# Writing the residual of an encoder layer to the output early, and adding the final feed-forward result to it by an accumulating DMA

## The chip, the cores and the metric

The kernel runs on the 8 cores of one Trainium2 chip, each core on its own part of the tokens with no exchange between them. The metric is the device time in microseconds of the slowest core. The profile is of one execution, taken on the slowest core of that execution (core 3).

## The reference

```
for l in range(2):                       # DEPTH
  h = rmsnorm(x, g_pre_mix);  u = h @ w_in[l]         # 1024 -> 6144
  y_a = pooled means of four windows, projected, scaled
  y_b = b_gate * dwconv3(c_gate * v)
  m = sigmoid(ga) * y_a + sigmoid(gb) * y_b
  x = x + rmsnorm(m @ w_out[l], g_post_mix)
  f = rmsnorm(x, g_pre_ffn)
  x = x + rmsnorm((silu(f @ w_ffn_gate) * (f @ w_ffn_up)) @ w_ffn_down, g_post_ffn)
```

This is applied to 2 sequences of 8192 tokens and 16 sequences of 2048 tokens, in fp32, with width 1024 and a hidden width of 2816. The rows that matter here are the last two: the residual x after the mixing half is used once to make f and once more at the very end, in the sum.

## The kernel before

Each core takes 6 tiles (the loop over t) of 1024 tokens, with a halo of 16 on either side: 1056 columns, held with the features on the 128 partitions in 8 chunks (k). For each tile both layers (l) are run in full on the chip. The columns are cut into three sub-tiles s of 352. x_t (fp32) holds the residual, h_t (bf16) the normalised input of the matmuls, o_t (fp32) the result of an output projection before its normalisation, m_t (bf16) the mixed values, and R the intermediate values. h_t and m_t are also used as scratch for the squares from which the norms are made.

One layer is: the projections of four groups g (for g = 0 four weight blocks are kept and s is the outer loop, lines 457 to 463), the output projection (lines 524 to 530, s outer), gate and up of the feed-forward (line 534 on; for its first three pairs of weight blocks s is the outer loop, lines 549 to 552, 12 groups of 8 matmuls for each s), and down. The last four column blocks of down (the "tail", lines 585 to 588) have s as the outer loop: 4 groups of 22 matmuls for each s.

Between two halves of a layer stand two chains for each s. chain_A (line 311) closes a half: 8 matmuls with a matrix of ones sum the squares in h_t (rstd_for), ScalarE makes the reciprocal root by Ln and Exp, VectorE multiplies the 8 chunks of o_t by it (mult_r), and VectorE and GpSimd add them to x_t (add_x). Then pre_sq writes the squares of x_t to m_t on ScalarE. chain_B (line 305) opens the next half: 8 matmuls with ones over m_t, Ln and Exp, and 8 scalar_tensor_tensor on VectorE that write h_t.

In the last layer of a tile (final) chain_A adds into o_t instead of x_t, and then, in this order: load_x issues the load of the next tile's x into the same columns of x_t (SP's queue), store_y issues the store of o_t to yout (SP's queue), halo_mask clears halo columns on VectorE (s = 0 and s = 2 only), pre_sq squares the new x, and chain_B is put off. So in the code before, the new x can be loaded only when the old residual has been added.

The chains are woven between the groups of matmuls by a list, pend. defer appends an entry with a number of matmuls to wait for; each main group calls run_pending, which looks at the first entry alone (line 212), runs it when its number has fallen to 0, and lowers the number of all entries by the size of the group. ensure_h(s) (line 206) is called ahead of each group that reads h_t: as long as any entry carries the tag s, it runs entries from the front of the list, whatever their numbers are. Each engine runs its instructions strictly in the order in which they were emitted; waits are semaphores that Sched works out from reads and writes.

The weights are fetched as fp32 and cast to bf16 by DMAs issued from GpSimd's queue into 11 slots; a load is emitted when the unit 11 places earlier is released (release, issue_upto). The tail of down holds 8 slots until rel_tail runs, 40 matmuls after it was deferred. Of the four blocks with which the next tile starts (pool, ga, v, gb), the first three are loaded ahead, and the fourth, gb, is emitted behind chain_A of s = 1.

Of the kernel before, what the change touches and what calls it, by code (L numbers as in the profile page):

```python
# [9 lines left out]
ALU = mybir.AluOpType  # L10
# [3 lines left out]
KC = 8  # L14
FF = 2816
JC = 22
DEPTH = 2
NT = 6
TV = 1024
HALO = 16  # L20
W = TV + 2 * HALO
NSUB = 3
SW = W // NSUB
# [78 lines left out]
def build_nc():  # L102
# [8 lines left out]
    yout = nc.dram_tensor("yout", [NT, 128, KC, TV], F32, kind="ExternalOutput").ap()  # L111

    with contextlib.ExitStack() as es:
# [3 lines left out]
        x_t = sb("x_t", [128, KC, W], F32)  # L117
        h_t = sb("h_t", [128, KC, W], BF16)
        o_t = sb("o_t", [128, KC, W], F32)
# [32 lines left out]
        def emit_all(S, plan, rec):  # L152
            X = [[Buf() for _ in range(NSUB)] for _ in range(KC)]
# [9 lines left out]
            SGB = [Buf() for _ in range(NSG)]  # L163
            CSB = Buf()
            MISC = Buf()

            state = {"bank": 0, "unit": 0, "ln": 0, "sg": 0, "issued": 0, "released": 0}
            pend = []
# [34 lines left out]
            def defer(nmm, fn, tag=None):  # L203
                pend.append([nmm, fn, tag])
# [82 lines left out]
            def load_x(t, s):  # L287
                S.dma("sp", (lambda q, t=t, s=s: q.dma_start(out=x_t[:, :, col(s)],
                                                             in_=xin[t, :, :, s * SW:(s + 1) * SW])),
                      ("xl", s), writes=[X[k][s] for k in range(KC)])  # L290

            def halo_mask(t, s):
                if s == 0:
                    bl = [X[k][0] for k in range(KC)]
                    tsmul(x_t[:, :, 0:HALO], x_t[:, :, 0:HALO], cc(128 + 2 * t), reads=bl + [CSB], writes=bl)
                if s == NSUB - 1:
                    bl = [X[k][NSUB - 1] for k in range(KC)]
                    tsmul(x_t[:, :, W - HALO:W], x_t[:, :, W - HALO:W], cc(128 + 2 * t + 1),
                          reads=bl + [CSB], writes=bl)

            def pre_sq(s):
                for k in list(range(KC // 2, KC)) + list(range(KC // 2)):
                    act(m_t[:, k, col(s)], x_t[:, k, col(s)], AF.Square, reads=(X[k][s],), writes=(M[k][s],))

            def chain_B(s, gbase):
                bi = rstd_for(s, lambda k, s_: m_t[:, k, col(s_)], M)
                for k in range(KC):
                    stt(h_t[:, k, col(s)], x_t[:, k, col(s)], cc(gbase + k), banks[bi][:, 0:SW], ALU.mult, ALU.mult,
                        reads=(X[k][s], BANKB[bi], CSB), writes=(H[k][s],))

            def chain_A(s, t, l, which):
                cb = l * 64
                bi = rstd_for(s, lambda k, s_: h_t[:, k, col(s_)], H)
                final = which == "ffn" and l == DEPTH - 1
                lo = max(s * SW, HALO)
                hi = min((s + 1) * SW, W - HALO)
                def mult_r(k):
                    tt(o_t[:, k, col(s)], o_t[:, k, col(s)], banks[bi][:, 0:SW], ALU.mult,
                       reads=(O[k][s], BANKB[bi]), writes=(O[k][s],))

                def add_x(k, eng):
                    if not final:
                        tt(x_t[:, k, col(s)], x_t[:, k, col(s)], o_t[:, k, col(s)], ALU.add,
                           reads=(X[k][s], O[k][s]), writes=(X[k][s],), eng=eng)
                    else:
                        tt(o_t[:, k, col(s)], x_t[:, k, col(s)], o_t[:, k, col(s)], ALU.add,
                           reads=(X[k][s], O[k][s]), writes=(O[k][s],), eng=eng)

                def store_y():
                    S.dma("sp", (lambda q, t=t, lo=lo, hi=hi: q.dma_start(  # L330
                        out=yout[t, :, :, lo - HALO:hi - HALO], in_=o_t[:, :, lo:hi])),
                          ("st", s), reads=[O[k][s] for k in range(KC)])

                for k in range(KC // 2, KC):
                    mult_r(k)
                    add_x(k, "pool")
                for k in range(KC // 2):
                    mult_r(k)
                    add_x(k, "dve")
                if which == "mix":  # L340
                    gnext = cb + 16
                    nt_ = t
                elif not final:
                    gnext = (l + 1) * 64
                    nt_ = t
                else:
                    if t + 1 >= NT:
                        store_y()
                        return
                    gnext = 0  # L350
                    nt_ = t + 1
                    load_x(nt_, s)
                    store_y()
                if which == "ffn":
                    halo_mask(nt_, s)
                pre_sq(s)
                defer(120 if final else 72, lambda: chain_B(s, gnext), tag=s)

            def out_proj_evac(bi, c, s, gbase):
                act(o_t[:, c, col(s)], banks[bi][:, 0:SW], AF.Copy, reads=(BANKB[bi], CSB), writes=(O[c][s],),  # L360
# [235 lines left out]
            while pend:  # L596
                it = pend.pop(0)
                it[1]()
            S.final_wait("sp", [("st", i) for i in range(NSUB)])

        rec = []
        emit_all(Sched(), None, rec)
# [145 lines left out]
```

How the kernel before makes its waits and increments, by code:

```python
        def run_stream(engine, name):  # L612
            for waits, fn, ikey, iamt in S.streams[name]:
                for key, val in waits:
                    engine.wait_ge(sems[key], val)
                if fn is not None:
                    ins = fn(engine)
                    ins.then_inc(sems[ikey], iamt)
```

## Time and profile before

| | |
|---|---|
| time, median of 2 runs | 6384.32 us (6290.19 and 6478.44) |
| time of the profiled execution | 6289.86 us |
| its span on core 3 | 6288.1 us (cores: 6258.3 to 6288.1) |
| TensorE busy | 5662.1 us, 90% |
| ScalarE / VectorE / GpSimd busy | 3278.4 / 2917.8 / 743.3 us |
| granted TensorE clock, mean | 0.953 |

Busy time is the time in which an engine had an instruction under way. A matmul at the full clock and one at half the clock both count as busy, so a stretch with a low granted clock looks busier than the work in it.

### The profile page before, as it was taken

The numbers are of one execution on the slowest core, as the hardware profiler recorded it, in microseconds if no ns is written. First come the engines' busy times: TensorE is split into PE (matmuls) and PEld (weight loads), VectorE is DVE, ScalarE is ACT, GpSimd is POOL, SyncE is SP. The second block draws the span as 40 slices with busy tenths as digits, with TensorE's granted clock in tenths as the row PEclk, the third lists the DMA queues.
The fourth block names the chain that finished last, engine by engine and source line by source line (L and its number), as shares of the span: only waits on it lengthen the run. The fifth ranks groups of instructions, "written<-read, shape, count | busy, mean of one in ns | idle before, by whom it ended". The sixth has DMA issues, their size and how long they took to land.

```text
span 6288.1 us, 107415 instructions; the slowest of 8 cores (6258.3 to 6288.1 us)
## 1 busy us (share of the span) xinstructions
PE 5662.1 (90%) x36864; PEld 3644.5 (58%) x36864; DVE 2917.8 (46%) x4934; ACT 3278.4 (52%) x6793; POOL 743.3 (12%) x1132
## 2 busy tenths in 40 slices
PE   6999998889989699998968999978899896999999
PEld 3566655556656365665645665645566563656655
DVE  5643542552553264265246436425525633643642
ACT  4564563465555356456435645635655553564564
POOL 0101011010110101101111011010101101011011
PEclk9999999899999899999989999989999997999999
DMA  5334343533434443343353343444334344433532
GB/s 102 63 63 72 62 67 82 92 59 64 74 52 75 100 76 58 58 84 61 65 101 60 63 73 62 68 91 84 61 58 79 60 70 99 68 63 61 84 57 62
DMA packets 159073, 448.39 MB, mean 71 GB/s; under 512 B 14032, under 2 KB 57040, under 8 KB 158544
## 3 DMA queue, kind: packets, MB, share of 16 engines
q0 software_dynamic: 120960, 390.12, 37.7%
q1 hardware_dynamic: 37584, 51.39, 2.5%
q8 instruction: 310, 5.08, 0.3%
q14 instruction: 219, 1.79, 0.1%
HBM read 806.36 MB, written 25.17 MB: 132 GB/s over the span
## 4 chain that ended last, share of the span: by engine, by line
PE 77%; DVE 9%; ACT 7%; DMA 4%; issue 3%; DVEq 0%; ACTq 0%; POOL 0%; SPq 0%; POOLq 0%
PE bank L227 77%; DMA x_t<-xin 4%; DVE o_t L242 4%; DVE h_t L246 3%; ACT m_t L238 2%; DVE x_t L242 2%; ACT sg L238 1%; ACT h_t L238 1%; ACT o_t L238 1%; ACT lnv L238 1%; ACT bank L238 1%; ACT R L238 0%; DVE R L242 0%; DVE m_t L242 0%; DVEq L615 0%
## 5 line engine op out<-in xcount | busy, mean ns | idle before, releaser
L227 PE MATMUL bank<-h_t,slot 128*128 128x352 bf16 x26496 | 4090.7, 318 | 484.9 <-ACT h_t L238 138.4
L227 PEld LDWEIGHTS bank<-h_t,slot 128*128 128x128 bf16 x26496 | 2623.1, 99 | 1935.3 <-issue 517.0
L227 PE MATMUL bank<-R,slot 128*128 128x352 bf16 x6912 | 1045.0, 313 | 0.0
L238 ACT ACTIVATE sg<-bank 128x352 f32<-128x352 f32 x1368 | 627.0, 458 | 529.1 <-DVE sg L242 428.0
L227 PEld LDWEIGHTS bank<-R,slot 128*128 128x128 bf16 x6912 | 676.5, 98 | 355.1
L238 ACT ACTIVATE sg<-sg,onef 128x352 f32<-128x352 f32 x1368 | 804.0, 588 | 128.5 <-ACT sg L238 2.6
L242 DVE TENSOR_TENSOR sg<-bank,sg 128x352 f32<-128x352 f32 x792 | 415.1, 524 | 966.6 <-ACT sg L238 960.2
L238 ACT ACTIVATE o_t<-bank,cs 128x352 f32<-128x352 f32 x576 | 326.2, 566 | 693.7 <-PE bank L227 693.7
L242 DVE TENSOR_TENSOR o_t<-o_t,bank 128x352 f32<-128x352 f32 x576 | 270.8, 511 | 815.6 <-ACT bank L238 815.6
L238 ACT ACTIVATE m_t<-x_t 128x352 bf16<-128x352 f32 x576 | 244.5, 486 | 709.2 <-DVE x_t L251 368.1
L242 DVE TENSOR_TENSOR R<-bank,R 128x352 f32<-128x352 f32 x576 | 281.4, 519 | 606.7 <-PE bank L227 573.9
L246 DVE SCALAR_TENSOR_TENSOR h_t<-x_t,cs,bank 128x352 bf16<-128x352 f32 x576 | 289.6, 575 | 550.4 <-ACT bank L238 522.4
L238 ACT ACTIVATE R<-bank 128x352 f32<-128x352 f32 x576 | 236.1, 461 | 549.6 <-DVE R L242 439.2
L242 DVE TENSOR_TENSOR R<-R 128x1055 f32<-128x1055 f32 (+5 forms) x384 | 428.0, 1115 | 69.3 <-ACT R L238 51.8
L242 DVE TENSOR_TENSOR R<-bank,sg 128x352 bf16<-128x352 f32 x792 | 415.7, 525 | 86.4 <-DVE sg L242 5.1
L238 ACT ACTIVATE sg<-sg 128x352 f32<-128x352 f32 x792 | 393.2, 496 | 74.5 <-ACT sg L238 2.2
L227 PE MATMUL bank<-m_t,slot 128*128 128x352 bf16 x2304 | 371.2, 324 | 50.5 <-DVE m_t L242 37.7
L227 PEld LDWEIGHTS bank<-m_t,slot 128*128 128x128 bf16 x2304 | 230.7, 101 | 187.1 <-issue 58.5
L242 POOL TENSOR_TENSOR x_t<-x_t,o_t 128x352 f32<-128x352 f32 x216 | 224.3, 1065 | 836.8 <-DVE o_t L242 836.8
L238 ACT ACTIVATE R<-sg 128x352 f32<-128x352 f32 x576 | 286.1, 497 | 56.9 <-ACT sg L238 2.2
L181 POOL DMA_DIRECT2D slot<-win x288 | 153.5, 540 | 1336.1 <-PE bank L227 1332.3
L181 POOL DMA_DIRECT2D slot<-wgu x264 | 140.4, 534 | 1397.1 <-PE bank L227 1396.9
(32 smaller groups left out, 1961.0 us busy)
## 6 DMA issues: line engine op xcount, KB each, us to landing
slot<-win POOLq DMA_DIRECT2D x288, 512.0 KB, 6.5
slot<-wgu POOLq DMA_DIRECT2D x264, 512.0 KB, 7.2
slot<-wdd POOLq DMA_DIRECT2D x192, 352.0 KB, 5.6
x_t<-xin SPq DMA_DIRECT2D x18, 1408.0 KB, 10.1
slot<-wod POOLq DMA_DIRECT2D x48, 512.0 KB, 5.6
yout<-o_t SPq DMA_DIRECT2D x12, 1344.0 KB, 13.3
yout<-o_t SPq DMA_DIRECT2D x6, 1408.0 KB, 12.4
slot<-pwd POOLq DMA_DIRECT2D x48, 128.0 KB, 4.0
```

The source lines that it names most:

```text
L181: g.dma_start(out=slots[si][:, 0:nel], in_=src_ap)),
L227: ins = pe.matmul(out_ap, lhsT=l_, rhs=r_, start=(i == 0), stop=(i == n - 1))
L238: a.activation(out=out, in_=in_, func=func, **kw)), reads=reads, writes=writes)
L242: v.tensor_tensor(out=out, in0=in0, in1=in1, op=op)), reads=reads, writes=writes)
L246: v.scalar_tensor_tensor(out=out, in0=in0, scalar=scalar, in1=in1, op0=op0, op1=op1)),
```

## The change

Once chain_B of s has made h_t for the feed-forward of the last layer, a new function after_mid stores x_t of that s to yout, loads the next tile's x into the same columns, and defers (by 220 matmuls, with no tag) the halo mask and the squares of the new x. chain_A of the last layer no longer adds x: it multiplies o_t and then issues, from GpSimd's queue, for each chunk k a DMA that adds o_t to yout in memory. chain_B of the next tile is deferred by 24 matmuls instead of 120. The other places are as before.

```diff
-            def chain_B(s, gbase):
+            def chain_B(s, gbase, after=None):
...
+                if after is not None:
+                    after()
+
+            def after_mid(s, t):
+                lo = max(s * SW, HALO)
+                hi = min((s + 1) * SW, W - HALO)
+                S.dma("sp", (lambda q, t=t, lo=lo, hi=hi: q.dma_start(
+                    out=yout[t, :, :, lo - HALO:hi - HALO], in_=x_t[:, :, lo:hi])),
+                      ("st", s), reads=[X[k][s] for k in range(KC)], writes=(YB[s],))
+                if t + 1 < NT:
+                    load_x(t + 1, s)
+
+                    def nxt(s=s, t=t):
+                        halo_mask(t + 1, s)
+                        pre_sq(s)
+                    defer(220, nxt)
...
+                if final:
+                    for k in range(KC):
+                        mult_r(k)
+                        S.dma("pool", (lambda g_, t=t, k=k, lo=lo, hi=hi: g_.dma_start(
+                            out=yout[t, :, k, lo - HALO:hi - HALO], in_=o_t[:, k, lo:hi], accum_op=ALU.add)),
+                              ("acc", k * NSUB + s), reads=[O[k][s], YB[s]], writes=())
+                    if t + 1 < NT:
+                        defer(24, lambda: chain_B(s, 0), tag=s)
+                    return
...
                 if which == "mix":
                     gnext = cb + 16
-                    nt_ = t
-                elif not final:
+                    aft = (lambda: after_mid(s, t)) if l == DEPTH - 1 else None
+                else:
                     gnext = (l + 1) * 64
-                    nt_ = t
-                else:
-                    if t + 1 >= NT:
-                        store_y()
-                        return
-                    gnext = 0
-                    nt_ = t + 1
-                    load_x(nt_, s)
-                    store_y()
-                if which == "ffn":
-                    halo_mask(nt_, s)
+                    aft = None
+                    halo_mask(t, s)
                 pre_sq(s)
-                defer(120 if final else 72, lambda: chain_B(s, gnext), tag=s)
+                defer(72, lambda: chain_B(s, gnext, aft), tag=s)
...
-            S.final_wait("sp", [("st", i) for i in range(NSUB)])
+            S.final_wait("sp", [("st", i) for i in range(NSUB)] + [("acc", i) for i in range(KC * NSUB)])
```

## Rows read from the trace of the kernel before

**Rows 1.** The page: busy time by engine, and the chain that ended last, by line.
```profile
PE 5662.1 (90%) x36864; PEld 3644.5 (58%) x36864; DVE 2917.8 (46%) x4934; ACT 3278.4 (52%) x6793; POOL 743.3 (12%) x1132
PE bank L227 77%; DMA x_t<-xin 4%; DVE o_t L242 4%; DVE h_t L246 3%; ACT m_t L238 2%; DVE x_t L242 2%; ACT sg L238 1%; ACT h_t L238 1%; ACT o_t L238 1%; ACT lnv L238 1%; ACT bank L238 1%; ACT R L238 0%; DVE R L242 0%; DVE m_t L242 0%; DVEq L615 0%
```

**Rows 2.** Windows, PE: start:end, us, busy (matmuls), clock, DMA share, GB/s.
```profile
1014.20:1150.20 136.00, 78.04 (x456) 0.77 0.44 102
...
5200.00:5330.00 130.00, 72.95 (x399) 0.75 0.46 105
```

**Rows 3.** Timeline, first tile boundary: start, us, engine, what, [idle before <-releaser].
```profile
1018.81 19.85 PE L227 MATMUL bank<-R,slot 128*128 128x352 bf16 x132
...
1069.21 5.37 PE L227 MATMUL bank<-h_t,slot 128*128 128x352 bf16 x24 [13.20 <-ACT h_t L238]
...
1088.53 0.54 SPq L288 DMA_DIRECT2D x_t<-xin  x1
...
1116.23 3.20 ACT L238 ACTIVATE m_t<-x_t 128x352 bf16<-128x352 f32 x8 [37.23 <-DVE x_t L251]
...
1119.92 2.51 PE L227 MATMUL bank<-h_t,slot 128*128 128x352 bf16 x8 [27.20 <-ACT R L238]
```

**Rows 4.** Timeline, layer 0 to layer 1 in the first tile, PE.
```profile
568.90 4.85 PE L227 MATMUL bank<-h_t,slot 128*128 128x352 bf16 x16 [6.19 <-ACT sg L238]
```

**Rows 5.** Timeline, start of the last layer's gate and up, first tile.
```profile
791.88 5.79 PE L227 MATMUL bank<-h_t,slot 128*128 128x352 bf16 x24 [6.26 <-ACT h_t L238]
...
797.50 1.36 PE L227 MATMUL bank<-m_t,ones 128*128 128x352 bf16 x8
...
800.17 4.02 DVE L246 SCALAR_TENSOR_TENSOR h_t<-x_t,cs,bank 128x352 bf16<-128x352 f32 x8 [0.62 <-ACT bank L238]
...
804.11 2.23 DVE L242 TENSOR_TENSOR o_t<-o_t,bank 128x352 f32<-128x352 f32 x5
...
813.62 5.16 PE L227 MATMUL bank<-h_t,slot 128*128 128x352 bf16 x24 [6.41 <-DVE sg L242]
```

**Rows 6.** Timeline, the same stretch: where the chains of s = 0 stand.
```profile
770.36 0.53 DVE L242 TENSOR_TENSOR x_t<-x_t,o_t 128x352 f32<-128x352 f32 x1
...
779.99 4.02 DVE L246 SCALAR_TENSOR_TENSOR h_t<-x_t,cs,bank 128x352 bf16<-128x352 f32 x8 [9.11 <-ACT bank L238]
```

**Rows 7.** The page: DMA queues (packets, MB, share) and issues (KB each, us to landing).
```profile
q0 software_dynamic: 120960, 390.12, 37.7%
q1 hardware_dynamic: 37584, 51.39, 2.5%
...
slot<-win POOLq DMA_DIRECT2D x288, 512.0 KB, 6.5
...
x_t<-xin SPq DMA_DIRECT2D x18, 1408.0 KB, 10.1
yout<-o_t SPq DMA_DIRECT2D x12, 1344.0 KB, 13.3
...
slot<-pwd POOLq DMA_DIRECT2D x48, 128.0 KB, 4.0
```

**Rows 8.** Timeline, end of the last tile, where no x is loaded.
```profile
6246.51 1.36 PE L227 MATMUL bank<-h_t,ones 128*128 128x352 bf16 x8
...
6249.18 2.25 DVE L242 TENSOR_TENSOR o_t<-o_t,bank 128x352 f32<-128x352 f32 x5 [56.35 <-ACT bank L238]
...
6262.03 10.01 PE L227 MATMUL bank<-R,slot 128*128 128x352 bf16 x66
...
6263.50 2.24 DVE L242 TENSOR_TENSOR o_t<-o_t,bank 128x352 f32<-128x352 f32 x5 [8.03 <-ACT bank L238]
...
6275.96 2.24 DVE L242 TENSOR_TENSOR o_t<-o_t,bank 128x352 f32<-128x352 f32 x5 [6.18 <-ACT bank L238]
```

**Rows 9.** Timeline, GpSimd's weight loads at the first tile boundary.
```profile
1054.43 0.57 POOL L181 DMA_DIRECT2D slot<-win  x1
...
1087.93 2.66 POOL L181 DMA_DIRECT2D slot<-win  x5
```

More of the change, by code:

```diff
@@ L165, in emit_all @@
             MISC = Buf()
+            YB = [Buf() for _ in range(NSUB)]
             state = {"bank": 0, "unit": 0, "ln": 0, "sg": 0, "issued": 0, "released": 0}
```

## The prediction

> **What bounds the kernel now.** I read the busy shares first: TensorE 90% busy, no other engine over 52% [rows 1]. So only idle TensorE time, and time at its lower clock, can be won. The chain of waits says where some of it is: 77% TensorE, and 4% the DMA that loads x [rows 1], some 250 us. Then I looked for TensorE's idle times in the timeline. They cluster where one tile ends and the next begins, five times in a run. The first boundary shows the pattern [rows 3]: x is loaded when the old residual has been added (for the third sub-tile its load is issued at 1088.5); ScalarE, which runs in order, stands in front of the squares of the new x while finished banks wait behind them, so TensorE stands for 13.2 us, and for 27.2 us at the third load, whose squares start 27.7 us after its issue. Restarted matmuls are slow: 8 in 2.51 us (0.31 us each), where 132 in a row take 19.85 us, thus (19.85 - 0.31)/131 = 0.149 us each [rows 3]. 352 columns in 0.149 us is the 2.4 GHz level and 0.31 is the 1.2 GHz one.
>
> The whole price of a boundary, idle time and slow clock together, is the length of a window around it less its matmuls at 0.149 us [rows 2]: 136 - 456 x 0.1492 = 68.0 for the first, 130 - 399 x 0.1492 = 70.5 for the fifth, and 67.7, 67.2 and 65.2 for the three between, which look the same. Sum **338.6 us**, 5.4% of the run.
>
> **Part 1: the boundary, -338.6 us.** In the changed kernel the squares of the new x are in m_t before the tail of down. The final chain_A is ones, Ln, Exp, 8 multiplications; it has no add, no squares and no DMA on which ScalarE or VectorE waits. For the timing I use the last tile, which ran without loads [rows 8]. Count from chain_A of s = 0 (ones at 6246.5, called 0): multiplications from +2.7 on; chain_A of s = 1 multiplies from +17.0; the last tail matmul ends at 6272.0, +25.5. The change puts two more ones groups of 1.36 us in here (chain_B of s = 0 and 1, each 2 groups of 22 behind its chain_A), so the next tile's matmuls start at +28.2. h_t of s = 0 must be ready then: its ones start at about +9.3, and from ones to the end of the 8 VectorE instructions is 800.17 + 4.02 - 797.50 = 6.7 us [rows 5], so +16. h_t of s = 1 is ready near +34, needed 8 groups (9.5 us) behind +28.2. For s = 2 chain_A comes after two groups and chain_B at the sixth; h_t is ready near +42, needed at +28.2 + 19.1 + 2.7 = +50. None is late. I take the whole 338.6 as gone and look for what is late next.
>
> **Part 2: GpSimd's queue.** 144 accumulating DMAs are added (8 for each s, 24 a tile), in the place of 72 adds on GpSimd and 72 on VectorE, which were beside TensorE's work. Each waits for its multiplication; five of these take 2.25 us [rows 8], eight 3.7, and the GpSimd adds in the same place waited for the same instructions, so the issue itself costs nothing. What matters is their time in the DMA queue, since the load of block gb is emitted right behind the eight of s = 1 (before, at 1054.4, behind the adds [rows 9]), and seven more loads behind the eight of s = 2. No row shows an accumulating DMA. Let T be the time of the eight (1.4 MB). Lower bound: plain copies, 51.39 MB in 2.5% of 6288 us over 36 DMAs [rows 7], **4.4 us**. Upper bound, if each trip ends before the next starts: 8 x 4.0 us, from the smallest load, pwd [rows 7], 32 us, or 64 us if the read of the destination and the write are a trip each. Deadlines: gb is needed 6 groups into the tile, +28.2 + 7.2 = +35.4, and with a landing time of 6.5 us [rows 7] it comes at +19.1 + T + 6.5; so it is in time up to **T = 9.8**. Above 15.6 the groups queue on each other: gb comes at 9.5 + 2T, late by 2T - 25.9; the block behind it (due at +28.2 + 28.6 + 2.7 = +59.5) adds T - 20.9. Together 3T - 46.8 a boundary. I take T = 8.8, twice the copy, as an accumulation reads two operands and writes one; that it is nearer the copy than the trips is because loads do overlap: five are issued in 2.66 us [rows 9], and 390.12 MB in 37.7% of the span is 3.2 us for the 0.52 MB of a win load, which takes 6.5 us to land [rows 7]. At T = 8.8 gb has 1.0 us to spare. Landing times scatter, so I allow 2.5 us a boundary: **+12.5 us**.
>
> The Trainium skill has a rule against many small DMAs ("DMA: Bandwidth & Descriptors", section on the anatomy of one DMA): about 2.0 us fixed plus bytes/436e3 us. Eight of 176 KB in series would be 19 us, late by 12 us a boundary, 60 us in all; the rows of overlapping loads speak against the series. The skill's "Collectives: The Full Stack" (Part 3, on the bandwidth ceiling) holds that a reduction costs two source reads on one ring and thus halves the rate, not that the add itself is slow, which would be T = 8.8; no row here shows it.
>
> **Part 3: the start of the last layer's gate and up, five tiles.** Here the list works against the change. When chain_B of s = 0 runs, after_mid appends an entry of 220 at the place ahead of chain_B of s = 1, and only the first entry is looked at. So chain_B of s = 1 does not run after 72 matmuls but when ensure_h(1) forces it, at the first group that needs it; ahead of it comes the deferred mask and squares. The same for s = 2. Before, chain_B had its slack (ones at 797.5, eight groups before s = 1) [rows 5]. Now: s = 0 restarts at 791.9 and has 88 matmuls left, 13.1 us plus 2.2 for the slow start (24 in 5.79 us), so it ends at 807.2. ScalarE finishes the last step's three activations (1.6), squares the new x (3.2 [rows 3]), makes the root (1.2), VectorE writes h_t (4.2 with its latency): 10.2 us, of which the two ones groups cover 2.6. **Stall 7.6.** Then chain_A of s = 2 comes right behind and blocks ScalarE's evacuations: in the rows TensorE is released 9.5 us after VectorE starts that chain (804.1 to 813.6) and has 7.2 us of free banks: **2.2**. At s = 2 again 10.2 less one ones group: **8.8**. Sum 18.6; the old stall of 6.41 goes [rows 5]. Net 12.2, and 1.9 for one more slow restart: **14.1 a tile, +70 us in five**. In the sixth tile nothing is deferred by 220 and nothing is lost.
>
> For the loads: the store of s = 0 can go out at 770.9, when the last add is done, and the load at 784, when chain_B has read x [rows 6] and the store (13.3 us [rows 7]) has landed; 10.1 us later it is there, 794, before 807. The load of s = 1 goes out near 817 and is there at 827, needed at 835. The third has 33 us. So SP's queue delays no one; 18 stores moved here and 25 MB of additional traffic find idle DMA engines, and the weight loads are issued from another queue. The other halo_mask and 72-matmul places stay. Two squares groups of 3.2 us move out of the boundary; that of s = 2 lies in steady gate-up work and costs nothing while ScalarE has spare time (1.6 us of activations for 2.4 us of matmuls).
>
> **Part 4: the end.** Before, the span ends 12.1 us behind the first of the last multiplications, at 6276.0 [rows 8], with the adds and one store between. Now the first accumulate goes 0.6 us behind it and the eighth lands some T + 4.0 us later (4.0 the landing of the smallest load [rows 7]): 13.4 for T = 8.8. I count 0 for it; T = 32 makes it +24, T = 64 +56.
>
> **Sum.** 6289.9 - 338.6 + 12.5 + 70 = 6034, **6035 us**, 4.1% under the profiled execution; that execution is the lower of the two runs, 1.5% under their median.
>
> **Rivals.**
> (a) The loads of x land late. If they take the 27 us of the third load in rows 3, the squares forced by ensure_h wait for 784 + 27 = 811, not 807, and for 844, not 835: some 4 + 9 us a tile beyond the sum, 65 us: **6100**. For it: gate-up weight loads are issued about then. Against: in the rows the long landing came with seven weight loads just issued.
> (b) The accumulates are slower than two copies, T = 19: 2 x 19 - 25.9 = 12 a boundary, **6085**. For it: rows of 1.4 KB, read and written. Against: the overlap above.
> (c) A chain remains at the boundary as between layers 0 and 1, where there is no load and TensorE still stands 6.2 us [rows 4] and restarts slowly: some 10 us five times, **6085**. Against: that stall is ScalarE waiting on adds for squares, which this boundary no longer has.
> (d) Each DMA of the eight waits for the one before, T = 32: 49 us a boundary eat the gain of 338.6/5 - 14.1 = 53.6: 6290 - 268.6 + 246 + 24, **6290**, no change.
> (e) On the other side: the read of yout and the write back are each a trip, T = 64, at the same place, GpSimd's DMA queue ahead of gb. 3 x 64 - 46.8 = 145 a boundary against 53.6: 6290 - 268.6 + 727 + 56, **6805**. It turns slower than before at T = 33, and slower by 2% at about T = 42.
>
> **Chances.** Forecast 0.56; (a) 0.13; (b) 0.12; (c) 0.05; (d) 0.07; (e) 0.07. Faster by over 2% (about what a measurement of this kernel can tell from no change): 0.86; within 2%: 0.07; slower: 0.07. The range goes from 5965, where the forced chains of part 3 cost almost nothing (the floor is 6290 - 339 = 5951), to 6200, which takes in (a), (b) and (c) together.
>
> **What would show it.** In the changed kernel's boundary windows the matmuls should fill the time at clock 1.00, with no wait for x_t. At the start of the last layer's gate and up TensorE should show two idle times of 7 to 9 us per tile, released by VectorE's h_t, with 8 squares of m_t just before Ln. The landing time of the accumulates gives T directly; if TensorE waits for a slot or a DMA 6 groups into a tile, (b), (d) or (e) is at work. If ScalarE's m_t waits for the load of x, it is (a). Wrong would be the reading that the load is what costs the 68 us, if the boundary stays above 15 us with neither of these.

## The result

The changed kernel's median is 6199.06 us of 11 runs (6012.7 to 6771.96), that of the kernel before, in the runs taken with it, 6617.88 us of 10 (6287.2 to 7198.04). The ratio of the two is 0.954, 95% interval 0.950 to 0.959. It is taken from runs in which the granted clock of TensorE was about the same on both dies; in the others it was lower on one die or both, whatever the kernel. The profiled execution took 6012.4 us, 277.5 less than that of before (6289.9). The sum of the prediction was 6034. As ratios of the profiled executions: 0.956 measured, 0.959 forecast.

Below, spans and windows are compared on cores whose clock was not lowered, and mostly by one stage: from the start of the output projection of layer 1 to that of layer 0 in the next tile. It holds both places that the change touches. In the changed kernel it begins and ends with the first and the last of these rows of the timeline; the middle one is the first matmul of down (start, us, engine, what, idle before):

```profile
747.45 2.80 PE L228 MATMUL bank<-m_t,slot 128*128 128x352 bf16 x9 [3.14 <-DVE m_t L243]
...
973.73 6.58 PE L228 MATMUL bank<-R,slot 128*128 128x352 bf16 x43
...
1241.96 8.25 PE L228 MATMUL bank<-m_t,slot 128*128 128x352 bf16 x43 [3.15 <-DVE m_t L243]
```

The difference is 494.5 us; the five stages of this profile take 494.1 to 494.5. In the kernel before they took 547.1 to 552.3, mean 549.6. So 55.3 us went from each of five stages, 276 us in all: the whole of what the spans differ by. The other stage, from layer 0 to layer 1, took about 496 us in both.

The first matmul of down parts the two places that the change touches. In the kernel before, the same two rows of the first of the five tiles read

```profile
748.27 11.98 PE L227 MATMUL bank<-m_t,slot 128*128 128x352 bf16 x68 [3.14 <-DVE m_t L242]
...
961.83 13.44 PE L227 MATMUL bank<-R,slot 128*128 128x352 bf16 x89
```

Output projection, gate and up took 213.0 to 213.7 us before and 225.9 to 226.3 after: 12.7 more a tile. Down and the boundary took 333.7 to 339.0 before, mean 336.2, and 268.2 or 268.3 after: 68.0 less.

### The profile page after: what moved, and what is told of

Its sections match the earlier page's. It is cut to its first block, busy times and chain, and to the rows that moved or that the text cites. A ratio compares the mean times of both kernels' runs of the same rounds, so it can differ in the third digit from the quotient of the medians.

```text
span 6010.9 us, 107550 instructions; the slowest of 8 cores (6009.1 to 6010.9 us)
## 1 busy us (share of the span) xinstructions
PE 5621.3 (94%) x36864; PEld 3633.8 (60%) x36864; DVE 2876.1 (48%) x4862; ACT 3281.8 (55%) x6793; POOL 795.5 (13%) x1204
## 3 DMA queue, kind: packets, MB, share of 16 engines
q0 software_dynamic: 141696, 415.30, 43.4%
## 4 chain that ended last, share of the span: by engine, by line
PE 83%; DVE 7%; ACT 6%; issue 2%; DMA 1%; ACTq 0%; DVEq 0%; POOL 0%; SPq 0%; POOLq 0%
PE bank L228 83%; DVE o_t L243 3%; DVE h_t L247 2%; ACT m_t L239 2%; DVE x_t L243 2%; ACT sg L239 1%; ACT h_t L239 1%; DMA x_t<-xin 1%; ACT o_t L239 1%; ACT lnv L239 1%; ACT bank L239 0%; DVE R L243 0%; ACT R L239 0%; DVE sg L243 0%; DVE m_t L243 0%
## 5 line engine op out<-in xcount | busy, mean ns | idle before, releaser
L228 PE MATMUL bank<-m_t,slot 128*128 128x352 bf16 x2304 | 372.0, 324 | 49.9 <-DVE m_t L243 37.7
L182 POOL DMA_DIRECT2D slot<-win x288 | 182.6, 860 | 1137.1 <-PE bank L228 1136.0
```

The lines of the kernel that those rows point to most:

```text
L182: g.dma_start(out=slots[si][:, 0:nel], in_=src_ap)),
L228: ins = pe.matmul(out_ap, lhsT=l_, rhs=r_, start=(i == 0), stop=(i == n - 1))
```

## The profile after

Busy shares, and the chain of work that ended last, by line. Against [rows 1] the load of x has fallen from 4% of the chain to 1%, and TensorE is busy 94% of the time.

```profile
PE 5621.3 (94%) x36864; PEld 3633.8 (60%) x36864; DVE 2876.1 (48%) x4862; ACT 3281.8 (55%) x6793; POOL 795.5 (13%) x1204
PE bank L228 83%; DVE o_t L243 3%; DVE h_t L247 2%; ACT m_t L239 2%; DVE x_t L243 2%; ACT sg L239 1%; ACT h_t L239 1%; DMA x_t<-xin 1%; ACT o_t L239 1%; ACT lnv L239 1%; ACT bank L239 0%; DVE R L243 0%; ACT R L239 0%; DVE sg L243 0%; DVE m_t L243 0%
```

Windows around the first and the last of the five tile boundaries (start:end, us, TensorE busy and matmuls, clock, DMA share, GB/s), to be held against [rows 2]:

```profile
1013.50:1149.50 136.00, 136.00 (x914) 1.00 0.76 112
...
4973.00:5109.00 136.00, 136.00 (x914) 1.00 0.75 112
```

136 us hold 914 matmuls at clock 1.00 where they held 456 at 0.77. 914 x 0.149 = 136: nothing of the 68 us is left, and the three boundaries between read the same (913 or 914 matmuls, clock 1.00). The price is seen in the timeline at the start of the last layer's gate and up:

```profile
791.08 15.33 PE L228 MATMUL bank<-h_t,slot 128*128 128x352 bf16 x88 [6.26 <-ACT h_t L239]
...
806.25 1.36 PE L228 MATMUL bank<-m_t,ones 128*128 128x352 bf16 x8
...
808.64 3.20 ACT L239 ACTIVATE m_t<-x_t 128x352 bf16<-128x352 f32 x8 [1.54 <-DVE x_t L252]
...
812.94 4.02 DVE L247 SCALAR_TENSOR_TENSOR h_t<-x_t,cs,bank 128x352 bf16<-128x352 f32 x8 [4.39 <-ACT bank L239]
...
817.11 17.15 PE L228 MATMUL bank<-h_t,slot 128*128 128x352 bf16 x96 [8.31 <-DVE h_t L247]
...
843.32 6.92 PE L228 MATMUL bank<-h_t,slot 128*128 128x352 bf16 x35 [7.86 <-DVE h_t L247]
```

s = 0 now runs through in 88 matmuls, then come the squares of the next tile's x (808.6), then the VectorE instructions of chain_B, then TensorE's first matmul of s = 1, 8.31 us late; at s = 2 it is 7.86. The old wait of 6.41 [rows 5] is gone. The window 780 to 880 holds 473 matmuls where that of before held 559.

GpSimd's queue at the first boundary: the eight accumulates of s = 1, the load of gb behind them, and the answer for this one load (min/median/max to landing):

```profile
1048.83 7.00 POOL L354 DMA_DIRECT2D yout<-o_t  x8 [8.44 <-DVE o_t L243]
...
1053.14 3.25 POOL L182 DMA_DIRECT2D slot<-win  x1
```
```profile
DMA to landing us min/median/max: 12.1/12.1/12.1
```

gb landed at 1065.2, the last of the eight accumulates at 1062.3. TensorE's tile began at 1057.3 and reached its seventh group, the first with gb, near 1066.8: in time by 1.6 us, where the prediction had 1.0.

The DMA queues (packets, MB, share) and the issues (KB each, median us to landing), against [rows 7]:

```profile
q0 software_dynamic: 141696, 415.30, 43.4%
...
slot<-win POOLq DMA_DIRECT2D x288, 512.0 KB, 7.4
...
x_t<-xin SPq DMA_DIRECT2D x18, 1408.0 KB, 8.2
...
yout<-x_t SPq DMA_DIRECT2D x12, 1344.0 KB, 5.6
yout<-o_t POOLq DMA_DIRECT2D x96, 168.0 KB, 6.9
```

The queue of the GpSimd DMAs was at work for 43.4% of 6010.9 = 2609 us, before for 37.7% of 6288.1 = 2371 us: 238 us for 18 groups, T = 13.2 us. Timed directly, the eight took 11.5 to 14.0 us from the first issue to the last landing, median 12.8. By the records of their own packets they took 199 us of the queue, 11.0 a group; the other 39 us are mostly weight loads, whose packets took longer beside them.

## The experiments

Each kernel is the changed one with the edit shown. Two theories stood against each other at first. Mine: the late load of x was the price of a boundary, and the order of the list is the price of the change. The rivals: the removed adds and squares were a good part of the 68 us, and traffic or the accumulates cost what is left.

**A list of its own.**

```diff
-                    defer(220, nxt)
+                    later.append([220, nxt])      # counted down in run_pending, not seen by ensure_h
```

> The mask and squares of the next x are kept in a list of their own, so that they neither stand ahead of the other entries nor are pulled forward by ensure_h; all else as in the changed kernel. Theory (order of the list): at the start of the last layer's gate and up the idle times of 8.3 and 7.9 us with their slow restarts go and the old one of 6.4 us returns; the price worked out for it was 60.6 us over five tiles, so 5952 us (5940 to 5965) in place of 6012. Rival (the stores and loads placed there cost the time by traffic, or the squares themselves do): 6000 us or more.

Measured: ratio to before 0.978 (0.971 to 0.985) on a chip where the clock was lowered often. On two cores whose clock was not, in another run than the profiled one, the span was 5943 and 5948 us (clock 0.976); undisturbed stages took 481.5 to 483.2 us, 12 less than the 494.3 of the changed kernel. The waits at gate and up are those of before again (core 7):

```profile
788.39 5.68 PE L233 MATMUL bank<-h_t,slot 128*128 128x352 bf16 x24 [6.26 <-ACT h_t L244]
810.03 5.11 PE L233 MATMUL bank<-h_t,slot 128*128 128x352 bf16 x24 [6.41 <-DVE sg L248]
```

494.3 - 481.7 = 12.6 a tile, 63 us in five. Output projection, gate and up take 213.2 to 214.9 us in the undisturbed stages of cores 0, 1, 6 and 7, mean 214.0, where the kernel before took 213.0 to 213.7, mean 213.4: the order of the list is the price, and the stores and loads placed there cost some 0.6 us a tile. Down and the boundary take 268.2 or 268.3, as in the changed kernel.

**The squares behind.** ensure_h runs the untagged entry behind the chain instead of ahead of it.

```diff
                 while any(it[2] == s for it in pend):
                     it = pend.pop(0)
-                    it[1]()
+                    if it[2] is None:
+                        held.append(it)
+                    else:
+                        it[1]()
+                for it in held:
+                    it[1]()
```

> The order of the list stays, so chain_B of s = 1 and 2 is still forced at its first use, but what ensure_h pulls forward with it (the squares of the next x) is emitted behind it, not ahead. Theory: each of the two idle times loses the 3.2 us of squares that stand ahead of Ln on ScalarE, 8.3 and 7.9 become about 5.1 and 4.7; 6.4 us a tile, 32 us in five: 5980 us (5970 to 5990). Rival (the squares are the whole cost): near 5952. Rival (waiting for the load of x is in it): the gain is above 32 us, since the wait goes too.

Measured: 6078.81 us at best. The two waits shrink, nearly as forecast, but a third one appears (core 1, the second of its five stages, whose clock was not lowered):

```profile
1822.62 9.79 PE L234 MATMUL bank<-h_t,slot 128*128 128x352 bf16 x56 [4.29 <-DVE h_t L253]
1836.61 8.92 PE L234 MATMUL bank<-h_t,slot 128*128 128x352 bf16 x40 [4.19 <-DVE sg L249]
1852.20 18.11 PE L234 MATMUL bank<-h_t,slot 128*128 128x352 bf16 x108 [5.48 <-DVE h_t L253]
```

4.29 + 4.19 + 5.48 = 14.0 against 16.2, and this stage took 494.0 us, as in the changed kernel: there are three idle times instead of two, so one slow restart more (my price for one was 1.9 us). Of the other two undisturbed stages one took 494.2 us; in the other the middle wait was 2.5 and the stage took 490.7. Run behind chain_B the squares hold up ScalarE's evacuations, and TensorE waits for a bank. My 5980 was too low: no clear gain; the wait changed its place.

**The squares of the next x in chain_A.** Store and load stay early; mask and squares are emitted in the final chain_A.

```diff
                     if t + 1 < NT:
+                        halo_mask(t + 1, s)
+                        pre_sq(s)
                         defer(24, lambda: chain_B(s, 0), tag=s)
```

> Store and load of x stay early; the mask and the squares of the next x are emitted in the final chain_A instead, and nothing is deferred by 220. Theory (what cost the 68 us of a boundary was that the squares waited for a load, not the 3.2 us of squares themselves): boundaries stay filled with matmuls except for up to 2 us at s = 2, and the list is free as in the kernel with a list of its own: 5952 to 5965 us. Rival (squares and chains at the boundary are a good part of the 68 us): the boundary shows 10 us or more of idle time and the run 6000 us or more.

Measured: 6172.34 us at best; cores 0 and 1, whose clock was not lowered, took 5996 and 6000 us, the stages 491.5 to 493.0, ten more than with the list of its own. The boundary shows why (core 1):

```profile
1026.64 1.35 PE L228 MATMUL bank<-m_t,ones 128*128 128x352 bf16 x8 [1.92 <-ACT m_t L239]
...
1059.01 2.51 PE L228 MATMUL bank<-m_t,ones 128*128 128x352 bf16 x8 [5.05 <-ACT m_t L239]
```

chain_B's ones wait for the squares, 1.9 and 5.1 us, and restart slowly. My 5952 to 5965 was missed, the rival's mark (10 us a boundary) reached: of the 68 us some 10 belong to squares at the boundary even when no load is waited for (down and the boundary take 277.3 to 278.5 us on core 1, against 268.2).

**The late load.** Accumulates and early store stay, the load of x waits for the multiplications, chain_B is deferred by 120.

```diff
+                        load_x(t + 1, s, after=[O[k][s] for k in range(KC)])
+                        halo_mask(t + 1, s)
+                        pre_sq(s)
+                        defer(120, lambda: chain_B(s, 0), tag=s)
```

> The residual is stored early and the accumulating DMAs stay, but the load of the next x waits until the final chain_A has multiplied o_t, as it did in the kernel before, with mask and squares behind it and chain_B deferred by 120; no adds. Theory (the late load is what a boundary costs): idle time returns nearly whole, 60 to 70 us a boundary, over the 5952 us of a kernel with a free list: 6250 to 6290 us. Rival (the removed adds, the store behind the load and the shorter deferral were a good part of the gain): below 6150 us.

Measured: 6303.49 us at best, cores from 6257 to 6302; stages of 546.6 to 547.8 and two of 535.8 and 538.8. The waits are back (core 5, first boundary), behind squares on ScalarE that wait for the load:

```profile
1072.44 3.20 ACT L239 ACTIVATE m_t<-x_t 128x352 bf16<-128x352 f32 x8 [25.17 <-DMA x_t<-xin]
...
1076.57 5.52 PE L228 MATMUL bank<-h_t,slot 128*128 128x352 bf16 x24 [20.04 <-ACT h_t L239]
...
1114.78 2.50 PE L228 MATMUL bank<-h_t,slot 128*128 128x352 bf16 x8 [14.54 <-ACT R L239]
```

547 against 549.6: without the adds, but with the late load, the change would be worth nearly nothing. Against the 481.7 of the list of its own it is 54 to 66 us a boundary, but some 10 of these are the squares at the boundary. The nearest kernel is the one with the squares in chain_A: against its 491.5 to 493.0 it is 43 to 56. Two things differ from it, the late load and chain_B's 120 matmuls instead of 24, and they were not tried apart; the two long waits shown, 34.6 us together, stand right behind squares that waited for the load.

**The changed kernel as a yardstick, and the accumulates taken away and tripled.**

> The changed kernel itself, beside the next three on the same chip, as their yardstick: 6012 us on a core whose clock is not lowered, 494.4 us from the output projection of layer 1 to that of the next tile's layer 0, as in its first profile.

Measured: 6194.94 us at best, the kernel before beside it 6310.70. On core 1 one stage took 494.3 and the other four 522.0 to 522.2, 27.8 more; on core 7 all five took 522. More of this below.

The plain write (GpSimd's DMAs overwrite yout, so the residual is missing from the output):

```diff
-                            out=yout[...], in_=o_t[:, k, lo:hi], accum_op=ALU.add)),
+                            out=yout[...], in_=o_t[:, k, lo:hi])),
```

> The 144 DMAs from GpSimd write o_t without adding it (the final sum with the residual is left out); all else as in the changed kernel. The trace of the changed kernel puts the eight DMAs of an s at about 13 us of the DMA queue, and the load of block gb landed 12.1 us after its issue, some 1.6 us before its first use, so the accumulates are just hidden. Theory: the same time within 5 us (6012), with the queue's share down and gb landing in 7 to 9 us. Rival (the accumulates cost something elsewhere, in gate and up or at the end): 6000 us or less. The issue on GpSimd's queue (0.87 us each) tells whether the accumulate makes the descriptors dearer: 0.53 as for a weight load if so.

Measured: stages of 521.9 to 522.2 (core 1) beside the yardstick's 522.0 to 522.2. The adding costs these stages nothing. But accumulates are dearer in themselves; queue and issue of the plain writes read

```profile
q0 software_dynamic: 128640, 415.30, 39.3%
...
yout<-o_t POOLq DMA_DIRECT2D x96, 168.0 KB, 2.5
```

and of the accumulates in the yardstick

```profile
q0 software_dynamic: 141696, 415.30, 42.0%
...
yout<-o_t POOLq DMA_DIRECT2D x96, 168.0 KB, 7.0
```

39.3% of 6303.1 less 2371 is 106 us, 5.9 for a group of eight; 42.0% of 6193.3 less 2371 is 230, 12.8 for a group. By this difference an accumulate takes 2.2 times a plain write from the same queue, but the difference also holds what the weight loads lost beside them. By the records of their own packets it is 10.6 us a group against some 4.2 (an estimate: part of the plain packets have the size of a weight load's), a factor of 2.5, and from the first issue to the last landing 13.3 against 6.5 at the median. The accumulates went out in 20736 more packets than the kernel before has, the plain writes in 7680. GpSimd's record of an issue is 0.85 us or longer against 0.54, yet the eight issues start 0.54 us apart in both. The Trainium skill says in "Collectives: The Full Stack" (Part 3, "The bandwidth ceiling") that the reduction of a collective runs at half the rate of a copy because it reads two sources. The factor here is 2.2 to 2.5; whether the reason is the same, or the smaller packets, is not shown here.

The accumulates tripled (two more, into scratch tensors, behind each):

```diff
+                        for i in range(2):
+                            S.dma("pool", (... out=ysc[i][...], in_=o_t[:, k, lo:hi], accum_op=ALU.add)), ...)
```

> Each accumulating DMA is done three times, the second and third into scratch tensors that are stored beside yout (two more stores for each s). T becomes about 40 us for an s. Theory (the DMA queue ahead of gb decides, 3T - 46.8 us a boundary): TensorE waits 60 to 75 us a boundary, beginning at the first group that uses gb: 6310 to 6390 us. Rival (only the issue on GpSimd's queue counts, 24 x 0.87 = 21 us ahead of gb): 15 to 20 us a boundary, 6090 to 6110 us. Rival (the margin is large): within 10 us of 6012.

Measured: 6450.80 us at best; undisturbed stages of 537 to 540 us on most tiles (534 to 544 in all), 43 to 46 more. TensorE waits for the weights, first at gb (core 4):

```profile
1125.69 23.39 PE L230 MATMUL bank<-h_t,slot 128*128 128x352 bf16 x144 [34.52 <-DMA slot<-win]
1155.77 9.39 PE L230 MATMUL bank<-h_t,slot 128*128 128x352 bf16 x48 [6.68 <-DMA slot<-win]
```

The queue took 45.9% of 6449.1 = 2960 us, so T was 32.7, not 40, for 24 DMAs; 3T - 46.8 gives 51 for it, and 43 to 46 were measured. The first of the two waits begins 6 groups into the tile. The place and the mechanism of rivals (b), (d) and (e) are right; the real T of 13 is only just too small to set them off.

**The squares apart.** On top of the list of its own, pre_sq is deferred instead of standing behind the adds.

```diff
-                pre_sq(s)
-                defer(72, lambda: chain_B(s, gnext, aft), tag=s)
+                def sq_then_b():
+                    pre_sq(s)
+                    defer(16, lambda: chain_B(s, gnext, aft), tag=s)
+                defer(56, sq_then_b, tag=s)
```

run_pending runs any entry that is due, ensure_h only those of its s.

> On top of the list of its own: pre_sq of every chain that is not final is deferred by 56 matmuls instead of standing right behind the adds, chain_B by 16 more, run_pending runs any entry that is due, ensure_h only those of its s. ScalarE then doesn't wait for the adds in front of filled banks. The kernel with the list of its own ran 5943 to 5948 us on cores with an undisturbed clock. It still stands 6.3 and 6.4 us at each of 12 starts of gate and up and 6.2 and 2.3 us at each of 6 starts of layer 1, with slow restarts behind them, 270 us together. Theory (ScalarE in order behind the adds is their cause): half or more of it goes, 5700 to 5810 us. Rival (chain_B comes too late and TensorE waits for h_t instead): 5900 us or more.

Measured: 5860.79 us at best, ratio to before 0.925 (0.910 to 0.941); spans of 5855 to 5860 us on all eight cores. The stages from layer 1 to layer 0 took 477.1 instead of 481.7, the others 485.6 instead of 495. 88 us under the list of its own, a third of the 270, not half. What is left is in part the rival's wait (core 1):

```profile
777.29 4.85 PE L235 MATMUL bank<-h_t,slot 128*128 128x352 bf16 x16 [4.96 <-DVE h_t L254]
795.62 4.67 PE L235 MATMUL bank<-h_t,slot 128*128 128x352 bf16 x19 [3.92 <-ACT m_t L246]
```

**The same kernels on one chip, and a deferral of 40.**

> The changed kernel once more, as the yardstick of this group. In its last profile the granted clock stood at 0.81 in full stretches of TensorE work that begin right behind the two idle times at gate and up and last some 170 us, 28 us for each; the first profile of the same kernel had none. Expected here: on each core 6011 us plus 28 for each such stretch. Theory (the idle times ahead of a full stretch bring it on): one in most tiles of this kernel, fewer in the kernels without these idle times. Rival (it belongs to the chip and the moment): all kernels of this group have about as many.

> The list of its own again, now with more rounds and beside the changed kernel. 5945 us on cores without a stretch of lowered clock, 66 us under the changed kernel. If the idle times bring the stretches on, it has fewer of them than the changed kernel; if not, as many.

> The squares apart again, as above: 5858 us where the clock is not lowered, about 0.932 of the kernel before. By the rival it has as many stretches of lowered clock as the others; its last profile had none on any core.

> As the squares apart, with pre_sq deferred by 40 matmuls instead of 56. In that kernel TensorE still waits 5.0 us for h_t of s = 1 at each of 12 starts of gate and up, and 4.0 us at the starts of layer 1: chain_B comes 16 matmuls (2.4 us) too late twice over. Theory: 2.4 us less at each of 18 places, and less of the slow restart, 5800 to 5830 us. Rival (ScalarE then waits for the adds in front of full banks again): 5850 us or more.

Measured, in this order: the changed kernel 6318.14 us at best; the list of its own 6036.59; the squares apart 5860.99, ratio 0.931 (0.925 to 0.938); deferred by 40, 5803.56 us, with all cores of its profile between 5795.8 and 5801.0 at a clock of 0.990 or 0.991. The waits for h_t are gone there; TensorE waits 1.9 to 3.7 us for the squares instead (stages of 472.4 and 480). The forecast of 5800 to 5830 holds where the clock is not lowered.

The first of these numbers matters for the change itself. The kernel before, in the same group, took 6301.70 us at best (median 6412.16 of 11), the changed kernel 6318.14 (median 6365.96 of 7): on this chip hardly anything of the gain was seen. The changed kernel's cores in its profile took 6144 to 6317 us where 6011 is undisturbed, with 5 to 11 times the 28 us; in its best run the cores of the kernel before took 6259 to 6300, close to their undisturbed 6258.

**Two idle times put back.**

```diff
+                    late = which == "mix" and l == DEPTH - 1 and s > 0
+                    defer(200 if late else BDEF, lambda: chain_B(s, gnext, aft), tag=s)
```

> As the squares deferred by 40, but in the last layer chain_B of s = 1 and 2 is deferred by 200 matmuls, so that ensure_h forces it at its first use, as in the changed kernel; two idle times of some 7 us a tile come back. Theory (an idle time right ahead of a long full stretch brings the lowered clock on): 5799 + 6 x 18 = about 5905 us on a core without a lowered stretch, and three or more stretches of 28 us on most cores, 5990 us or more. Rival (they belong to the chip and the moment, or to something else in the changed kernel): about 5905 us and as few lowered stretches as in the kernel beside it.

> The squares deferred by 40 once more, beside the run above and with more rounds: 5799 us on cores without a lowered stretch, and by either theory no more than one such stretch on most cores; about 0.922 of the kernel before.

Measured: the idle times are back, 5.48 and 8.04 us before these rows (core 7),

```profile
789.52 10.65 PE L235 MATMUL bank<-h_t,slot 128*128 128x352 bf16 x56 [5.48 <-DVE h_t L254]
815.36 34.83 PE L235 MATMUL bank<-h_t,slot 128*128 128x352 bf16 x206 [8.04 <-DVE h_t L254]
```

and cost 83 us in six tiles (5889 against 5806 us, core 7 of both; 70 to 90 on the others), 14 a tile. It took 5923.72 us at best, the kernel beside it 5838.03; that one's ratio to before is 0.930 (0.927 to 0.933). No stage of either profile, on any core, shows the 28 us step. But the lowered clock is in both, in stretches of 15 us and less (core 1, the kernel with the idle times put back first, start:end, us, TensorE busy and matmuls, clock, DMA share, GB/s):

```profile
839.00:853.00 14.00, 14.00 (x79) 0.81 1.02 152
```
```profile
802.00:816.00 14.00, 14.00 (x80) 0.81 0.58 181
```

On core 7 these add up to 153 us against 76, which at 0.81 of the clock is some 14 of the 83 us. So the two idle times alone did not bring the long stretches on here. That they have no part in them is not shown: the changed kernel was not run beside these two, and it may be that nothing had the long stretches that hour. They are not needed either: the list of its own has no forced idle times, and four of the five stages of core 5 in its first profile took 509 us and more instead of 481.7.

## Why the prediction was right, and where it was wrong

**The boundary.** Right: 338.6 us worked out, 5 x 68.0 = 340 measured, and the windows of after hold nothing but matmuls. The late load shows that this is in the main the load's doing: with it (and chain_B deferred by 120) 43 to 56 us a boundary return on top of the squares' 10. That some 10 of the 68 belonged to the squares was not in my working; it made no difference, since the change moves them too.

**GpSimd's queue.** The mechanism was right, T was too small (8.8, measured 12.8 to 13.2). The 4.4 us for a plain copy was about right (4.2 by the packets of the plain writes), but an accumulate is not two but 2.5 of them, and the weight loads beside it slow down too. By my own deadline of 9.8 such a T is 3 us late; gb was in time by 1.6 us. So the deadline was too tight by some 5 us and T too small by 4, two errors that cancelled, which is luck. On my own count from the first ones (1029.5), gb was needed at +37.3 and not at +35.4, as two groups of ones stand among the tile's first matmuls; and it landed 3.0 us behind the last accumulate, not 6.5, as it was already under way beside them. The allowance of 12.5 us was not needed. Rival (b)'s T of 19 and rival (d)'s 32, eight trips in series, are refuted by T; that they would hurt is shown by the tripled accumulates.

**The order of the list.** Forecast 14.1 a tile; 12.6 by the list of its own. The waits were to be 7.6, 2.2 and 8.8 us and were 8.31, none and 7.86. The middle one failed: the chain of s = 2 holds ScalarE up for as long as worked out, but TensorE had the 96 matmuls through in one piece; the experiment with the squares behind shows it is a near thing (2.5 to 4.2 us there).

**Rival (a)**, late loads of x: loads land in 8.2 us at the median, and in the changed kernel no wait of TensorE at gate and up ends with one. **Rival (c)**, a chain left at the boundary: none is.

**The sum.** 6034 against 6012.4 for the profiled execution: 22 too high, of which 12.5 are the allowance and 7 the smaller price of the list.

**What failed is the last step**, from the sum to the time. The sum starts from one execution of the kernel before, 6289.9 us, in which no core had a stretch at 0.81 of the clock. I wrote that this execution is the lower of two runs, 1.5% under their median, and left it there: no term and hardly any range for a run in which the clock is lowered. The medians are made of such runs. That of the kernel before was 6384.32 in two runs and 6617.88 in ten; that of the changed kernel is 6199.06, at the very edge of my range, where it owes its place to how many of the 11 runs were lowered (five took 6012.7 to 6014.4). 0.954 of 6617.88 would be 6315, outside the range. In the run of 6199.06 us four cores took 6010 to 6013 us at a mean clock of 0.972, the other four 6169 to 6197 at 0.937 to 0.942.

The term that was missing is measured in the later groups of runs: 28 us for each long stretch of lowered clock on a core (522.1 - 494.3). The changed kernel had 4 to 7 of them on the cores of one profile (6117 to 6193 us against 6011) and 5 to 11 in another. Nor may it be left out as common to both kernels: in the second of these groups it took nearly all of the gain. What decides how many a kernel gets stays open.

## What to carry to other kernels

When a load must wait for a buffer, ask what the last reader of the buffer is and whether a late small use (here the residual's add) can be done elsewhere; the load's date moved by half a layer and, with the squares behind it, 68 us a tile went. When entries are put into a list of which only the first is looked at, each one delays all behind it: an entry with a long count belongs in a list of its own. On an engine that runs in order, put work that waits for another engine behind the work that doesn't; moving the squares gave 88 us in six tiles, and 16 matmuls less of deferral 59 more.

A sum of waits is made against one execution. Before it is called the time, see how far the runs of the same kernel lie apart, and whether the change can alter that.

## What the runs showed of the hardware

The granted clock has a third value beside the levels of 1.2 and 2.4 GHz. In the yardstick's profile, core 1, a window inside a full stretch of TensorE work reads

```profile
900.00:920.00 20.00, 20.00 (x113) 0.81 0.27 45
```

113 matmuls in 20 us, 0.177 us each instead of 0.147. By the clock records this stretch goes from 848.2 to 1008.8 us, at 0.812 all along, with no idle time in it; behind it the clock is 1.00 again though TensorE had not paused. It begins 5.9 us after the clock came back from the 1.2 GHz level, behind the wait of 7.85 us at gate and up. In the three profiles with the most of them (the changed kernel twice, the list of its own once) all 136 stretches of 158 to 162 us begin 3 to 8 us after such a return. A return alone is not enough: the first profile of the changed kernel has 54 on each core, that of the kernel before 70 to 73, and neither has a long stretch.

The Trainium skill, "TensorE: Matmul & The Clock Gate" (Part 1, "Seeing it yourself", the warning on the peak-current limiter), has a limit that takes a die to 13/16 of the clock (0.8125); the 0.81 agrees. It does not agree for these stretches that the whole die goes together: they come in pairs of cores (cores 0 and 1 took 6144 to 6146 us, cores 2 and 3 of the same die 6245 in one run). In other runs all four cores of a die were slow together (6866 to 6891 us beside 6008 and 6011 on cores of the other die). Nor does it agree that all cores at dense work must run at it: the first profile of the changed kernel ran its boundaries at 1.00, and all eight cores have a mean of 0.972.

How often it happens differed by kernel in a way I did not expect and cannot explain. On one chip, over seven runs, the best core of the changed kernel was 133 us or more over 6011 in six of them, about five stretches; the best core of the squares apart, which uses TensorE more densely, was within 2 us of 5857 in all seven of its runs, though in two of these a die took 6613 to 6827. Idle times at gate and up alone are not the cause, as shown above. Whether it takes the dense stretches of several cores falling together was not tried. It stays open.
